# Moving the weight-splitting steps of the next head inside one head of a gated linear attention, on VectorE and ScalarE

## The reference

```python
q, f_fwd, f_bwd, i, z = _split_cols(h @ w_in, C_SIZES)      # five projections, 16 heads each
f = lb + (1.0 - lb) * jax.nn.sigmoid(f_pre)                 # per direction
k, lf = 1.0 - f, jnp.log(f)
...
b = jnp.cumsum(lf, axis=2)                                  # decay along time
o = einsum(q * exp(b), S) + sum over s <= t of q_t k_s exp(b_t - b_s) v_s
...
y = (rms(o_fwd + o_bwd) * silu(z)) @ w_out
```

## Time and profile before

| what | value |
|---|---|
| median of 3 runs | 2472.4 us |
| profiled execution, its own time | 2472.4 us |
| span of its trace | 2470.8 us |
| TensorE matmuls busy | 2302.9 us, 93% |
| VectorE busy | 1697.4 us, 69% |
| ScalarE busy | 1104.4 us, 45% |
| mean granted TensorE clock | 0.961 |
| heads 0 to 15 of section C, first L2610 to last | 1907.9 to 2390.5 us |

### The profile page before, as it was taken

One profiled execution on the slowest core, in us unless ns is written; L12 is line 12 of the kernel. 1 busy time (PEld: TensorE's weight loads), 2 busy tenths in 40 slices (PEclk: granted clock), 3 DMA queues, 4 the chain that ended last, 5 costly groups with the idle time before them and its releaser, 6 DMA issues.

```text
span 2470.8 us, 37763 instructions
## 1 busy us (share of the span) xinstructions
PE 2302.9 (93%) x13692; PEld 1998.4 (81%) x13692; DVE 1697.4 (69%) x3262; ACT 1104.4 (45%) x1761; POOL 88.9 (4%) x140
## 2 busy tenths in 40 slices
PE   7999889997999989996999999999996999999979
PEld 7998679996998769995777778888885888888868
DVE  6787858777877957785444554443544888888884
ACT  4433353334433254444555543333423666665552
POOL 0000000000000000001112201101100000000000
PEclk9999889998999989998999998999998999999989
DMA  7554126644654216553334431211211222222212
GB/s 279 214 202 162 69 90 216 229 171 161 220 203 179 80 66 221 197 194 80 78 74 76 74 97 66 72 60 62 84 69 51 86 85 85 85 84 78 85 51 102
DMA packets 81765, 298.62 MB, mean 121 GB/s; under 512 B 10132, under 2 KB 10644, under 8 KB 80916
## 3 DMA queue, kind: packets, MB, share of 16 engines
q1 hardware_dynamic: 77904, 284.72, 32.8%
q0 software_dynamic: 2048, 4.20, 3.0%
q10 hardware_dynamic: 1736, 8.67, 0.9%
HBM read 296.51 MB, written 1.05 MB: 120 GB/s over the span
## 4 chain that ended last, share of the span: by engine, by line
PE 38%; DVE 12%; issue 2%; ACT 1%; DVEq 0%; ACTq 0%
PE ps L711 29%; PE ps L1303 2%; DVE work L2644 2%; DVE work L2633 2%; DVE wsplit L1965 2%; PE ps L1162 1%; PE ps L1044 1%; PE ps L1058 1%; PE ps L1034 1%; DVE work L2683 1%; DVE work L2614 1%; DVE work L2612 1%; PE ps L1014 1%; PE ps L1281 1%; DVE work L2617 0%
## 5 line engine op out<-in xcount | busy, mean ns | idle before, releaser
L711 PE MATMUL ps<-hsplit,wsplit 128*128 128x256 f32 (+1 forms) x8280 | 1380.9, 325 | 39.1 <-DVE work L2654 17.0
L711 PEld LDWEIGHTS ps<-hsplit,wsplit 128*128 128x128 f32 x8280 | 1201.1, 192 | 170.9 <-issue 30.5
L1359 ACT ACTIVATE wsplit<-ring 128x1024 fp32r<-128x1024 f32 x465 | 490.9, 1057 | 644.6 <-PE ps L711 462.6
L1965 DVE TENSOR_TENSOR wsplit<-ring,wsplit 128x1024 fp32r<-128x1024 f32 x465 | 569.1, 1226 | 283.8 <-ACT wsplit L1359 271.4
L753 PE MATMUL ps<-wsplit,fsplit 128*128 128x512 f32 x1056 | 262.2, 398 | 19.7 <-DVE wsplit L1965 14.2
L753 PEld LDWEIGHTS ps<-wsplit,fsplit 128*128 128x128 f32 x1056 | 196.4, 192 | 58.4 <-DVE wsplit L1965 14.9
L2013 DVE SCALAR_TENSOR_TENSOR work<-ring,cs,work 128x128 f32<-128x128 f32 x672 | 206.1, 348 | 9.0
L2119 DVE SCALAR_TENSOR_TENSOR work<-work,vec 128x256 f32<-128x256 f32 x240 | 100.9, 479 | 1.7
L1456 ACT ACTIVATE work<-ps 128x256 f32<-128x256 f32 x88 | 33.7, 383 | 152.1 <-PE ps L711 152.1
L711 PEld LDWEIGHTS ps<-wsplit,hsplit 128*128 128x128 f32 x768 | 96.2, 199 | 5.3 <-issue 3.8
L711 PE MATMUL ps<-wsplit,hsplit 128*128 128x256 f32 x768 | 97.8, 291 | 1.1 <-DVE wsplit L1965 1.1
(11 more groups left out here) (321 smaller groups left out, 2319.7 us busy)
## 6 DMA issues: line engine op xcount, KB each, us to landing
ring<-panels SPq DMA_DIRECT2D x539, 512.0 KB, 4.2
work<-latent_weights ACTq DMA_DIRECT2D x2, 2304.0 KB, 13.7
work<-rpb POOLq DMA_DIRECT2D x64, 64.0 KB, 6.5
cst<-constants ACTq DMA_DIRECT2D x1, 1408.0 KB
work<-x SPq DMA_DIRECT2D x1, 1024.0 KB, 5.5
work<-post_rows ACTq DMA_DIRECT2D x2, 512.0 KB, 4.9
cT<-ctx ACTq DMA_DIRECT2D x1, 1024.0 KB, 8.6
out<-xT SPq DMA_DIRECT2D x1, 1024.0 KB, 3.9
```

What stands on the lines that cost most here:

```text
L711: ins = mm(out_, w(a), x(b), start=start and n == 0, stop=stop and n == 2, **kw)
L1359: af(wsplit[:, split_slot(name, n), 0, :], ring[:, p % slots, :], ACT.Copy).then_inc(high_ready, 1)
L1965: tt(parts[:, 1, :], ring[:, p % slots, :], parts[:, 0, :].bitcast(fp32), ALU.subtract)\
```

## The change

Three of the five `low` of a head, and one `high`, change their place on their engines. On ScalarE `high` of panel +1 moves from the head of `c_head` to behind the exponentials that end at `c_kh_ready`, and the wait for `c_b_ready` moves up ahead of the wait for `c_w_ready`. On VectorE `low` of +1 moves from behind L2626 to behind the eight L2644; `low` of +2 from between L2633 and L2644 to behind the output of head h-1; `low` of +3 from ahead of L2664 to behind it. No instruction is added or removed, and TensorE's and SyncE's programs are untouched.

```diff
 def c_head(h, par, n0, nx, more=True, before=True):        # ScalarE
-    high("C", 0, nx[0] + 1, nx[1])
     if before:
         c_square(h - 1)
...
     sigmoid(c_s[:, :, :], c_s[:, :, :]).then_inc(c_qz_sig, 1)
+    act.wait_ge(c_b_ready, h + 1)
     act.wait_ge(c_w_ready, h + 1)
     A.did(af(c_kh[:, 0, :], ...))
     af(c_kh[:, 1, :], ...).then_inc(c_kh_ready, 1)
+    high("C", 0, nx[0] + 1, nx[1])
     act.wait_ge(panels_used, n0 + 5)
     af(c_vT, ps[:, 3, :], ACT.Copy).then_inc(c_vT_ready, 1)
-    act.wait_ge(c_b_ready, h + 1)
     af(c_qs[:, :, :], c_b[:, :, 0:T], ACT.Exp).then_inc(c_eb_ready, 1)
...
                                                            # VectorE
     tt(c_bx[:, :, :], c_b[:, :, :], c_x[:, :, :], ALU.add).then_inc(c_w_ready, 1)
-    low("C", 0, nx[0] + 1, nx[1])
...
     ins.then_inc(c_aq_ready, 1)
-    if more:
-        low("C", 0, nx[0] + 2, nx[1])
     dve.wait_ge(c_w_ready, h + 1)
...
     ins.then_inc(c_ak_ready, 1)
+    low("C", 0, nx[0] + 1, nx[1])
     if before:
         c_output(h - 1, 1 - par)
+    if more:
+        low("C", 0, nx[0] + 2, nx[1])
...
         .then_inc(c_qs_ready, 1)
-    if more:
-        low("C", 0, nx[0] + 3, nx[1])
     dve.wait_ge(c_eq_ready, h + 1)
     tt(c_aq[:, :, :], ..., c_aq[:, :, :], ALU.mult).then_inc(c_q_ready, 1)
+    if more:
+        low("C", 0, nx[0] + 3, nx[1])
     if more:
         low("C", 0, nx[0] + 4, nx[1])
```

## The result

The changed kernel takes 2553.74 us (median of 4 runs, 2552.17 to 2561.17; the profiled execution took 2549.53 us) against 2471.5 us before (median of 4 runs); the ratio is 1.0341 with a 95% interval of 1.0318 to 1.0364. The forecast was 2553 us in a range of 2519 to 2574.

What follows compares the result with a forecast made beforehand. Heads were bound by two nearly full engines, TensorE (96%) and VectorE (88%), in a 31.75 us cycle. Order 50.4, head 0 1.1 and clock 29 us sum to 80.5: 2472.4 + 80.5 = 2553 us, range 2519 to 2574.

Steps and rivals of the forecast that it cites:

- closed loop: One head's cycle, L2610 through L2654, panels +2 and +3 and L1281 to the next head: 35.35 us against 31.75.
- signs: Expected in the changed kernel: TensorE's waits on `low`, L2654's wait gone, head near 37.4 us, clock near 0.91, VectorE idle.
- The order term: Heads 1 to 14: late `low` of +1 lengthens the cycle by 3.60 us a head, 50.4 us in all.
- The new wait: TensorE at panel +1, waiting for `low`: 13.51 - 8.57 = 4.9 us a head.
- Head 0: First head, where the clock was low and TensorE late: panels +2 and +3 begin 1.1 us later.
- Head 15: Head without projections: L1264's wait for L1880 grows 1.05 us, hidden by L1281's wait for L2606; cost 0.
- The clock term: Heads 1 to 14: a low stretch in every head slows TensorE's work by 2.1 us, 29 us in all.
- The clock that stays up: Rival: the clock does not fall, or rarely, in the new waits; 2524 us, chance 0.13.
- The low stretch that runs through the transposes: Rival: low clock over panel +1 and the transposes, 5.4 us a head, 76 us in all; 2600 us, chance 0.05.
- Faster: Rival: the wait for L2654 goes and nothing replaces it, at most 17.0 us; 2455 us, chance 0.04.
- no change: Rival: TensorE's need for panel +1 is hidden, the cycle stays at 31.75 us; 2472 us, chance 0.03.
- Covers: The other moves, costed at nothing because their results still land early; smallest cover 1.6 us, for `low` of +3.

Runs made afterwards that it cites:

- low1_between: The changed kernel with VectorE's `low` of +1 between the two groups of eight subtractions, 2.76 us earlier: 2489.61 us, ratio 1.0062.
- scalar_back: The changed kernel with ScalarE's program as it was before the change: 2556.19 us, ratio 1.0328.
- low3_back: The changed kernel with `low` of +3 alone put back ahead of L2664: 2555.35 us, ratio 1.0323.
- low2_only: The kernel before with only `low` of +2 moved, to behind the output of head h-1: 2474.51 us, ratio 1.0.
- fill16: The changed kernel with 16 added matmuls, results unread, on TensorE just ahead of panel +1: 2524.32 us, ratio 1.0196 to the kernel before.
- fill8: The changed kernel with 8 added matmuls, results unread, on TensorE just ahead of panel +1: 2530.9 us, ratio 1.0232.
- scalar_only: The kernel before with ScalarE's moves alone: 2509.47 us, ratio 1.0147.
- low23_only: The changed kernel with ScalarE's program and `low` of +1 back as before, leaving the moves of `low` of +2 and +3: 2490.46 us, ratio 1.0081.

## Why the prediction was right

**The chain.** The forecast's closed loop held step by step. `low` of +1 begins 12.22 us into the head (12.24 forecast), TensorE starts at 13.50 (13.51), the state product follows panels +2 and +3 after 5.84 (5.85), and the wait for L2654 is gone. Two of the signs that the prediction named came out a little off. The 14 waits are 4.34 to 4.63 us, 62.6 us in all, and not 4.6 to 4.9 us and 65 to 70; and the low stretch of head 1 begins behind its wait and not inside it. The granted clock of 0.91 and the 37.4 us from one L2611 to the next came as named, and so did VectorE's idle time ahead of `low` of +3. low1_between shows that the place of +1 carries most of the cost, scalar_back and low3_back that the moves of `high` and of +3 are covered, and low2_only that the move of +2 costs nothing even without the late `low` of +1.

**The order term** was 14 x 3.60 = 50.4 us and measured 14 x 3.33 = 46.6 us. The step that was off is the one from the transposes to panels +2: I had taken 0.44 + 0.60 = 1.04 us; in fill16 it is 2212.66 - 2211.88 = 0.78, since the next matmuls start 0.35 us after L1273 begins. The new wait was 4.62 us in every second head, where I had 4.9, and 4.36 us in the others: I put the twelve matmuls of the half panel at 0.233 us each, 2.80 us in all, and they end 3.12 us after they begin. This does not touch the cycle, which runs over `low`.

**Head 0** cost 34.8 us against the 33.9 of before, 0.9 us, forecast 1.1. **Head 15** cost 0, as forecast: L1264 waits 2 us longer for L1880 than in the earlier trace rows, and L1281 still waits for the output of head 14.

**The clock term** was 14 x 2.1 = 29 us, measured 14 x 2.48 = 34.7 us. It was the mis-sized term of the sum. That a fall would come in each head, and that the work under it is all on the path, was right. The size was off because the low stretch began some 3.2 us into a wait of 4.36 or 4.62 us, not 2.7 us into one of 4.9, so that 1.1 to 1.5 us of it were spent waiting and not 2.2. Head 1, with its shorter stretch, lost only 1.6 us. The two errors have opposite signs, 3.8 us too much for the order and 5.7 us too little for the clock: 46.6 + 0.9 + 34.7 = 82.2 us, against 80.5 forecast and 82.3 in the two traces. That 2553 came so near to 2553.74 is in part luck.

**The rivals.** The clock that stays up (2524 us) is what fill16 made, at 2524.32; that figure holds the 2.7 us which its added matmuls cost in head 0, where there is no wait of that length to fill, so the two agree so closely by chance. The low stretch that runs through the transposes did not happen: the clock is back at 2218.3, before the transposes begin. So nothing here bears on what the Trainium skill (TensorE: Matmul & The Clock Gate, Part 4: PE-mode transpose) says, that transposes do not count as busy for the clock in the way that matmuls do. Faster and no change are excluded by the interval.

**Covers** were costed rightly for the full change only. The 1.6 us that I gave `low` of +3 (1.4 measured: it ends at 2223.36, and TensorE has done panel +2 at about 2221.63 + 3.12 = 2224.75) exist because TensorE is 3.3 us late; without that delay the same move brings a wait of 1.06 us and costs 1.3 us a head, and ScalarE's 2.1 us a head come out as well. Costs that are hidden behind one late step are not free, they are only second.

## What to carry to other kernels

When a step moves back in an engine's order, count from a fixed point of the loop both when its result will land and when the consumer will ask for it; here that gave the new cycle to 0.3 us a head. A wait on TensorE can cost more than its length once the clock falls in it or behind it, and the slow work must be priced as well: here 2.5 us on top of 3.3, for a wait of 4.5. A move that is covered by another one's delay should be tried by itself before it is called harmless, and the move that paid here was the one that brings forward the release in which the cycle ends, the bank of q and z.

## What the runs showed of the hardware that was not expected

How often the clock fell to 0.50 in heads 1 to 14, by the waits that TensorE had in a head:

| run | waits in a head, us | heads with a fall |
|---|---|---|
| after | 4.34 to 4.63 | 14 of 14 |
| fill8 | 2.54 to 2.84 | 7 of 14 |
| low1_between, the longer wait | 1.86 to 1.88 | 3 of 6 |
| low1_between, the shorter wait | 1.59 to 1.61 | 0 of 8 |
| scalar_only | 0.9 to 1.2, then 1.9 | 4 of 14 |
| low23_only | 0.95 to 1.25, then 1.06 | 0 of 14 |
| before | 1.09 to 1.37 | 0 of 14 |
| fill16 | 0.74 to 1.03 | 0 of 14 |

Falls did not need waits as long as the 2.5 us that the prediction had seen: 1.9 us were enough in some heads. The fall could also come after the wait, while TensorE was already at work again (in fill8 up to 1.4 us after it). What a fall costs depends on its place: in fill8, with 3.41 us at 0.50 and all of it on panel +1, this panel took 7.2 us (2238.00 to 2245.21); in the changed kernel, with 6.83 us of which 1.1 were spent waiting, it took 8.25.

In fill16 the clock of heads 1 to 14 stayed up on matmuls whose results nobody reads, and these cost nothing where they fitted into the wait. They took 3.79 us of the 4.4 and made the kernel 1.2% faster than without them (2524.32 against 2553.74 us), although they cost 2.7 us in head 0.
